# Attention in a hybrid block: one kind of score area for large query tiles, one for small ones, and the two kinds in turn

## What is computed

```python
def block(args):                      # one block of queries
    q_blk, c_blk = args
    s = jnp.einsum('bqhcd,bkhcd->bchqk', q_blk, k) * scale
    mask = cid[None, :] <= c_blk[:, None]
    p = jax.nn.softmax(jnp.where(mask, s, NEG_INF), axis=-1)
    w = p[:, 0] - lam * p[:, 1]
    return jnp.einsum('bhqk,bkhe->bqhe', w, v)
```

## Time and profile before

| | us |
|---|---|
| median of 3 timed runs | 2460.54 |
| lowest, highest of them | 2460.26, 2462.5 |
| profiled execution, span | 2463.3 |
| attention in it | 351.0 to 567.0 |
| TensorE busy, whole span | 2234.1 (91%) |
| VectorE, ScalarE, GpSimd busy | 776.3, 475.8, 308.1 |

### The profile page before, as it was taken

How to read it: one execution, slowest core, us unless ns; L and a number is a source line. 1 busy time by engine, 2 the same in 40 slices (tenths; PEclk the granted TensorE clock), 3 DMA queues, 4 the chain that set the end, 5 groups by cost and what they waited for, 6 DMA issues and landing times. The chain is left out here.

```text
span 2463.3 us, 33586 instructions
## 1 busy us (share of the span) xinstructions
PE 2234.1 (91%) x13475; PEld 1269.7 (52%) x13475; DVE 776.3 (32%) x1637; ACT 475.8 (19%) x884; POOL 308.1 (13%) x263
## 2 busy tenths in 40 slices
PE   5999978889968999999976999999986999999994
PEld 4687535565545455455533555555544555545541
DVE  5652026554352111111116344444233111111116
ACT  2222114341110000000003344442110000001001
POOL 5343000001101111101003000000100101111102
PEclk9999988789978999999988999999987999999997
DMA  4100010002229999989979211102118999998987
GB/s 152 36 4 32 17 71 1 1 1 57 72 104 390 419 419 420 419 335 406 412 298 310 93 39 38 38 19 54 52 51 350 413 419 420 420 389 353 417 369 293
DMA packets 148201, 529.82 MB, mean 215 GB/s; under 512 B 43875, under 2 KB 66947, under 8 KB 131665
## 3 DMA queue, kind: packets, MB, share of 16 engines
q1 hardware_dynamic: 119232, 490.78, 50.4%
q0 software_dynamic: 13312, 33.84, 3.6%
q10 hardware_dynamic: 15504, 3.08, 0.6%
HBM read 499.99 MB, written 39.98 MB: 219 GB/s over the span
## 5 line engine op out<-in xcount | busy, mean ns | idle before, releaser
L1787 PE MATMUL l_main_pgu<-l_w_ring,l_ex_xT 128*64 128x256 f32 (+1 forms) x4992 | 472.8, 384 | 12.7 <-DMA l_w_ring<-in_l_moe_w_gate 9.5
L1787 PEld LDWEIGHTS l_main_pgu<-l_w_ring,l_ex_xT 128*64 128x64 f32 (+1 forms) x4992 | 285.2, 128 | 189.6 <-issue 40.5
L1833 PE MATMUL l_main_py<-l_w_ring,l_ex_hT 128*64 128x512 f32 (+1 forms) x1248 | 231.9, 595 | 1.9 <-DVE l_ex_hT L1904 1.9
L1784 PE MATMUL l_main_pgu<-l_w_ring,l_ex_xT 128*128 128x512 f32 x384 | 170.1, 596 | 4.8 <-DMA l_w_ring<-in_l_moe_w_gate 4.8
L2245 PE MATMUL lru_pr<-h2T,lru_wz 128*128 128x352 f32 (+1 forms) x480 | 144.3, 461 | 11.6 <-ACTq L2300 11.6
L1900 DVE TENSOR_TENSOR l_ex_hid<-l_ex_sil,l_main_pgu 128x256 f32<-128x256 f32 (+1 forms) x76 | 35.2, 463 | 376.9 <-PE l_main_pgu L1787 279.7
L1904 DVE COPY l_ex_hT<-l_main_ph 128x256 f32<-128x256 f32 (+1 forms) x76 | 35.4, 466 | 366.4 <-PE l_main_ph L1808 366.4
L2263 PE MATMUL lru_pg<-h2T,lru_wz 128*128 128x512 f32 x320 | 148.7, 592 | 0.0
L1833 PEld LDWEIGHTS l_main_py<-l_w_ring,l_ex_hT 128*64 128x64 f32 (+1 forms) x1248 | 69.1, 127 | 132.1 <-issue 124.8
L2245 PEld LDWEIGHTS lru_pr<-h2T,lru_wz 128*128 128x128 f32 x480 | 92.6, 193 | 64.4 <-ACTq L2300 12.0
L1876 ACT ACTIVATE l_ex_sil<-l_main_pgu 128x256 f32<-128x256 f32 (+1 forms) x76 | 31.7, 417 | 468.9 <-PE l_main_pgu L1787 373.2
(11 more groups left out here) (450 smaller groups left out, 2785.2 us busy)
## 6 DMA issues: line engine op xcount, KB each, us to landing
l_w_ring<-in_l_moe_w_gate SPq DMA_DIRECT2D x64, 2048.0 KB, 24.4
l_w_ring<-in_l_moe_w_up SPq DMA_DIRECT2D x64, 2048.0 KB, 30.5
l_w_ring<-in_l_moe_w_down SPq DMA_DIRECT2D x64, 2048.0 KB, 32.5
l_y<-expert_rows SPq DMA_DIRECT2D x32, 512.0 KB, 8.3
h_rows<-H SPq DMA_DIRECT2D x24, 512.0 KB, 5.2
lru_wz<-in_l_w_in SPq DMA_DIRECT2D x20, 512.0 KB, 5.0
H<-h_rows SPq DMA_DIRECT2D x16, 512.0 KB, 10.1
w_in<-in_l_w_in SPq DMA_DIRECT2D x3, 2048.0 KB, 8.1
```

What stands on the lines that cost most here:

```text
L1784: last = pe.matmul(out[:], x[:, k, :], w[0][:, k, :], start=k == 0, stop=k == KD - 1)
L1787: last = pe.matmul(out[HALF * h + o:HALF * h + o + m, 0:256], x[:, k, it.at + o:it.at + o + m], w[n][:, k, 256 * h:256 * h + 256], start=k ...
L1833: last = pe.matmul(py[b][HALF * h + o:HALF * h + o + m, :], hT[:, c % 2, HALF * (c // 2) + o:HALF * (c // 2) + o + m], ws[n][:, c, 512 * h ...
```

## The change

- The units are put in a new order: a list of wide units (tiles 4 to 8 in heads 0 and 2, 8 to 5 in heads 1 and 3) and a list of narrow ones (3 to 0, and 0 to 4) are dealt in turn, 18 of each.
- PSUM is divided anew: one area of two maps by 1024 columns for the units of even number, one of two maps by 512 columns for those of odd number. Scores of u now wait for both exponentials of u-2.
- Keys over an area's end (tile 8 in a wide area, tile 4 in a narrow one) go to the last 16 columns of the other area, beside the scores of the unit before, whose keys don't reach so far. TensorE does this ahead of that unit's scores; VectorE copies them out ahead of that unit's minima. Six units have such a tail, where four had one before.
- The waits around the tail in the bank `weighed` go.
- Of a tailed unit ScalarE takes the tail's exponential first.
- Lambda is made behind the first unit's minima and exponentials.

The orders of turn, weigh, copies, output and square against each other are as before.

```diff
-    WIDE, PER = 1024, 4
-    units = [(hd, qi) for hd in range(HEADS - 1) for qi in range(NT)] + [(HEADS - 1, qi) for qi in reversed(range(NT))]
+    WIDE, NARROW, PER = 1024, 512, 4
+    wide = [(hd, qi) for hd in range(HEADS) for qi in ((4, 5, 6, 7, 8) if hd % 2 == 0 else (8, 7, 6, 5))]
+    narrow = [(hd, qi) for hd in range(HEADS) for qi in ((3, 2, 1, 0) if hd % 2 == 0 else (0, 1, 2, 3, 4))]
+    units = [unit for two in zip(wide, narrow) for unit in two]
     U = len(units)
+    room = [(WIDE, NARROW)[u % 2] for u in range(U)]
+    keys = [sum(TILES[qi]) for _, qi in units]
+    held = [min(n, r) for n, r in zip(keys, room)]
+    tailed = [n > r for n, r in zip(keys, room)]
...
-        S = [ctx.enter_context(nc.psum_tensor(f"scores{i}", [P, WIDE], F32)) for i in range(3)]
+        S = [ctx.enter_context(nc.psum_tensor(f"scores{i}", [P, 2, n], F32)) for i, n in enumerate((WIDE, NARROW))]
...
+        tail_place = lambda u, m: S[(u - 1) % 2][0:m, :, room[u - 1] - N_META:room[u - 1]]
...
             def scores(u):
-                if u:
-                    pe.wait_ge(exp_done, 2 * u - 1)
-                if n > WIDE and u > LAG + 1:
-                    pe.wait_ge(o_copied, u - LAG - 1)
...
+                if u >= 2:
+                    pe.wait_ge(exp_done, 2 * u - 2)
+                if u >= 2 and tailed[u - 1]:
+                    pe.wait_ge(tail_done, tails[u])
+                if u + 1 < U and tailed[u + 1]:
+                    tail_scores(u + 1)
...
+            def tail_scores(u):
...
+                for c in range(2):
+                    pe.matmul(place[:, c, :], K.qT[rows[c], hd, q0:q0 + m], K.kT[rows[c], hd, h:n], start=True, stop=False)
+                for c in range(2):
+                    pe.matmul(place[:, c, :], hide[rows[c], 0:m], ones[rows[c], 0:n - h], start=False, stop=True).then_inc(tail_made, 1)
...
-                if j == 0 and tails[min(u + LAG + 2, U)]:
-                    pe.wait_ge(tail_done, tails[min(u + LAG + 2, U)])
...
         @block.scalar
-            act.wait_ge(lam_ready, 2)
-            act.activation(lexp[:], ldot[:], ACT.Exp).then_inc(lexp_done, 1)
...
+                if u == -1:
+                    act.wait_ge(lam_ready, 2)
+                    act.activation(lexp[:], ldot[:], ACT.Exp).then_inc(lexp_done, 1)
...
         @block.vector
+            def copy_tail(u):
+                m = TILES[units[u][1]][1]
+                dve.wait_ge(tail_made, 2 * tails[u + 1])
+                dve.wait_ge(s_ready, 2 * u)
+                if tails[u]:
+                    dve.wait_ge(exp_done, 2 * last_tail(u) + 2)
+                dve.tensor_copy(tail_sb[0:m, :, :], tail_place(u, m)).then_inc(tail_done, 1)
+                dve.wait_ge(tail_done, tails[u + 1])
...
             for u in range(-1, U + LAG + 1):
+                if u + 2 < U and tailed[u + 2]:
+                    copy_tail(u + 2)
                 if u + 1 < U:
                     minimum(u + 1, 0)
                     minimum(u + 1, 1)
+                if u == -1:
+                    difference()
                 if 0 <= u < U:
                     combine(u)
```

More of the change, by code:

```diff
@@ L657, in attention @@
     ms_ready, sd_ready, on_ready, oT_ready, oT_copied, g_ready = map(sem, ("ms_ready", "sd_ready", "on_ready", "oT_ready", "oT_copied", "g_ready"))
-    WIDE, PER = 1024, 4
-    units = [(hd, qi) for hd in range(HEADS - 1) for qi in range(NT)] + [(HEADS - 1, qi) for qi in reversed(range(NT))]
+    WIDE, NARROW, PER = 1024, 512, 4
+    wide = [(hd, qi) for hd in range(HEADS) for qi in ((4, 5, 6, 7, 8) if hd % 2 == 0 else (8, 7, 6, 5))]
+    narrow = [(hd, qi) for hd in range(HEADS) for qi in ((3, 2, 1, 0) if hd % 2 == 0 else (0, 1, 2, 3, 4))]
+    units = [unit for two in zip(wide, narrow) for unit in two]
     U = len(units)
+    room = [(WIDE, NARROW)[u % 2] for u in range(U)]
+    keys = [sum(TILES[qi]) for _, qi in units]
+    held = [min(n, r) for n, r in zip(keys, room)]
+    tailed = [n > r for n, r in zip(keys, room)]
+    assert U == HEADS * NT and not tailed[0]
+    assert all(keys[u] <= room[u] + N_META and keys[u - 1] <= room[u - 1] - N_META for u in range(U) if tailed[u])
     groups = [-(-(qi + 1) // PER) for _, qi in units]
     first_group = [sum(groups[:u]) for u in range(U + 1)]
-    tails = [sum(qi == NT - 1 for _, qi in units[:u]) for u in range(U + 1)]
+    tails = [sum(tailed[:u]) for u in range(U + 1)]
+    last_tail = lambda u: max(v for v in range(u) if tailed[v])
     with ExitStack() as ctx:
-        S = [ctx.enter_context(nc.psum_tensor(f"scores{i}", [P, WIDE], F32)) for i in range(3)]
+        S = [ctx.enter_context(nc.psum_tensor(f"scores{i}", [P, 2, n], F32)) for i, n in enumerate((WIDE, NARROW))]
         tp = ctx.enter_context(nc.psum_tensor("turned_w", [P, PER, P], F32))
         out_bank = ctx.enter_context(nc.psum_tensor("weighed", [P, 512], F32))
-        po, tail = out_bank[:, 0:P], out_bank[:, P:P + 2 * N_META].rearrange("p (c n) -> p c n", c=2)
+        po = out_bank[:, 0:P]
+        tail_place = lambda u, m: S[(u - 1) % 2][0:m, :, room[u - 1] - N_META:room[u - 1]]
         block = ctx.enter_context(nc.Block())
@@ L691, in cuts @@
             q0, m = TILES[units[u][1]]
-            n = q0 + m
-            ends = list(range(0, n, 512)) + [n]
-            return q0, m, n, list(zip(ends, ends[1:]))
+            return q0, m, keys[u], held[u]
         @block.tensor
@@ L698, in _ @@
             pe.wait_ge(hide_made, 4)
+            rows = [slice(64 * c, 64 * c + 64) for c in range(2)]
             def scores(u):
                 hd, qi = units[u]
-                q0, m, n, parts = cuts(u)
-                if u:
-                    pe.wait_ge(exp_done, 2 * u - 1)
-                if n > WIDE and u > LAG + 1:
-                    pe.wait_ge(o_copied, u - LAG - 1)
-                rows = [slice(64 * c, 64 * c + 64) for c in range(2)]
-                if n > WIDE:
-                    for c in range(2):
[L711 to L720, removed]
+                q0, m, n, h = cuts(u)
+                if u >= 2:
[4 more added lines that the diff above has]
+                    tail_scores(u + 1)
+                seen = n - 64 if qi else n
+                ends = list(range(0, h, 512)) + [h]
+                for a, b in reversed(list(zip(ends, ends[1:]))):
+                    lo = max(a, seen)
+                    for c in range(2):
+                        last = pe.matmul(S[u % 2][0:m, c, a:b], K.qT[rows[c], hd, q0:q0 + m], K.kT[rows[c], hd, a:b], start=True, stop=lo >= b)
                         if lo >= b and a == 0:
@@ L724, in scores @@
                         for c in range(2):
-                            last = pe.matmul(place(c, lo, b), hide[rows[c], 0:m], ones[rows[c], 0:b - lo], start=False, stop=True)
+                            last = pe.matmul(S[u % 2][0:m, c, lo:b], hide[rows[c], 0:m], ones[rows[c], 0:b - lo], start=False, stop=True)
                             if a == 0:
                                 last.then_inc(s_ready, 1)
+            def tail_scores(u):
+                hd, qi = units[u]
+                q0, m, n, h = cuts(u)
+                place = tail_place(u, m)
+                for c in range(2):
+                    pe.matmul(place[:, c, :], K.qT[rows[c], hd, q0:q0 + m], K.kT[rows[c], hd, h:n], start=True, stop=False)
+                for c in range(2):
+                    pe.matmul(place[:, c, :], hide[rows[c], 0:m], ones[rows[c], 0:n - h], start=False, stop=True).then_inc(tail_made, 1)
             def turn(u, j):
@@ L771, in _ @@
                 for h in range(HEADS):
-                    last = pe.transpose(S[i % 2][:, P * h:P * h + m], o_sb[0:m, i, P * h:P * h + P], K.ident[0:m, 0:m])
+                    last = pe.transpose(S[i % 2][:, 0, P * h:P * h + m], o_sb[0:m, i, P * h:P * h + P], K.ident[0:m, 0:m])
                 last.then_inc(oT_ready, 1)
@@ L804, in exps @@
                 act.wait_ge(mn_ready, x + 1)
-                s, prob, kw = S[x % 3], probs[u % PROBS][c], dict(bias=mn[0:m, x % 4:x % 4 + 1], scale=-1.0)
-                if n <= WIDE:
-                    act.activation(prob[0:m, 0:n], s[0:m, 0:n], ACT.Exp, accum_out=l[0:m, u % PROBS, c:c + 1], **kw).then_inc(exp_done, 1)
-                else:
-                    act.activation(prob[0:m, 0:WIDE], s[0:m, :], ACT.Exp, accum_out=l2[0:m, tails[u] % 2, c, 0:1], **kw)
-                    act.activation(prob[0:m, WIDE:n], tail_sb[0:m, c, :], ACT.Exp, accum_out=l2[0:m, tails[u] % 2, c, 1:2], **kw).then_inc(exp_done, 1)
+                s, prob, kw = S[u % 2], probs[u % PROBS][c], dict(bias=mn[0:m, x % 4:x % 4 + 1], scale=-1.0)
+                if not tailed[u]:
+                    act.activation(prob[0:m, 0:n], s[0:m, c, 0:n], ACT.Exp, accum_out=l[0:m, u % PROBS, c:c + 1], **kw).then_inc(exp_done, 1)
+                else:
+                    act.activation(prob[0:m, h:n], tail_sb[0:m, c, :], ACT.Exp, accum_out=l2[0:m, u % PROBS, c, 1:2], **kw)
```

(27 more changed lines are left out.)

6 lines of the change are left out of this document (3 added, 3 removed).

## The result

The kernel after takes 2475.8 us (median of 4 runs, 2471.4 to 2477.5) against 2460.9 us; the ratio is 1.0062 [1.0048, 1.0076]. I had forecast 2452 us. The second rival had 2474 us. Executions of one and the same kernel differ too, in most by up to 14 us, and they are longer where the granted clock, as a mean over the whole span, is lower: of 60 of the kernel before the shortest span is 2451.6 us at 0.949, the longest 2465.1 us at 0.942. One of the ten executions of after_fill took 5953.7 us at a granted clock of 0.41; the ratio leaves it out.

What follows compares the result with a forecast made beforehand. TensorE was taken to bound the attention loop, waiting mostly for turned-weight copies. Walk to 532.0 us plus 15 for the clock gave loop end 547.0 against 555.6, -8.6 us, so 2452 us; range 2440 to 2472.

Steps and rivals of the forecast that it cites:

- The second rival: Heavy pairs: output copy behind ScalarE's second exponential idles TensorE, clock stays 1.2 GHz, costing 37 us: 2474 us; chance 0.28.
- What bounds the loop: Attention loop: 19.6 us of TensorE waits for turned-weight copies outweigh the 5.8 us, outside the start, that a second area removes.
- Start: Loop start: lambda later puts scores of units 0 to 2 before 360.5 us; unit 4's scores end at 373.5.
- The walk of the pairs at full clock: Steady loop at 2.4 GHz: nine pair periods sum to 83.6 us, 41.8 per head against 40.6 before; no gain.
- The pair walked as 8.3 us: Lighter loop pair, wide units of 784 then 912 keys, ScalarE owning the first copy: 8.3 us per period.
- the one walked as 7.0: First of the nine walked loop periods, c = 4 in tile numbers: 7.0 us.
- The new wait of the weighing: Loop: weighing waits for the narrow unit's output copy behind ScalarE's second exponential, 1 us and over, about ten times.
- Drain: Loop end: the last units have 656 and 528 keys, taking 15 us against about 8 before.
- Clock: Loop: TensorE's clock drops behind idle stretches, six falls of 2.5 us, 15 us in all; bounds 8 and 37.
- The grant below 0.75 over the loop: Sign that the forecast is wrong: TensorE's granted clock below 0.75 over the whole attention loop.
- The first, no change: Loop: clock's share is 18 to 28 us as lighter pairs fall too; 2455.5 to 2465 us, middle 2460; chance 0.30.
- The third: Much faster: all waits hung on the areas, TensorE runs dense, 18 pairs of 6.9 us: 2406 us; chance 0.04.

Runs made afterwards that it cites:

- after_fill: Kernel after plus 26 unread float32 matmuls on TensorE ahead of the second turns of wide units, in their waits: 2454.0 us, ratio 0.9971.
- order_only: Kernel before with only the new order of units; its three areas, tails and start stay: 2495.7 us, ratio 1.0123.
- after_out_early: Kernel after with ScalarE's output copy ahead of the second exponential instead of behind it: 2462.0 us, ratio 1.0015.
- after_lambda_first: Kernel after with lambda made ahead of the first minima, as in the kernel before: 2480.8 us, ratio 1.0082.

## Why the prediction was wrong

- *What bounds the loop, and that its order is the matter*: right. Waits for the turned copy, not for areas; order_only shows it by itself (35.1 us of waits for the copy, 19.6 before).
- *Start*: right. Unit 4's scores end at 373.8 us (373.5); taking the edit out raises the median by 5 us, a size that the intervals leave uncertain.
- *The walk of the pairs at full clock*: nearly right. The pair walked as 8.3 us takes 8.9 (from 436.7 to 445.6), the one walked as 7.0 takes 7.6 (from 470.0 to 477.6); the turn and the weighing of the heavy pair are within 0.4 us. The new wait of the weighing was named, as 1 us and over some ten times; it came six times, 0.55 to 1.24 us, 5.4 us in all.
- *Drain*: walked as 15 us, measured 23.8, at a grant of 0.57. At 1.00, in after_fill, it takes 17.6 us, so the walk was 2.6 us short and the clock cost 6:
```profile
529.20:546.80 17.60, 13.68 (x86) 9.68 (x84) 10.52 (x37) 7.37 (x23) 0.00 (x0) 1.00 0.00 0
```
- *Clock*: **this is the step that failed**, "I take six falls of 2.5 us", 15 us. There are twelve falls, and most last 7 us, two of them 17 and over 20. Fifteen periods took 177.7 us where the walk has 143.5, and the drain adds 8.8: together 43 us over the walk in place of 15, and 547.0 + 28 is the measured 575.2. In these stretches 102 us ran at half. At the 0.33 us for each that after_fill gives, the clock's share is about 34 us; the other 9 are the walk, too short at full clock as the pairs and the drain above show. The 0.35 us for each that I took for the old loop was about right: what was wrong is how often and how long the grant falls. I had counted the idle stretches nearly right (ten of 1.6 us or more) and then let four of them pass without a fall; the control in my own sum, that the old loop had lost 21 us behind shorter waits, should have weighed more. I had let the 5 us of unbroken work behind a fall end it at once, when the row for 499 to 503 us showed half clock in a stretch of unbroken work. The grant below 0.75 over the loop, which I had named as a sign of being wrong, came (0.73).
- *Rivals*: the second gave the time (2474) and nearly the clock's share (37 us for some 34), and in after_out_early its mechanism is shown for 12 to 14 us. But it put the whole on the output copy. The runs put more on the waits for the turned copy: filling these is worth 22 us with the output copy left where it is. The first, no change, put the clock at 18 to 28 us and ended at 2465, too low. The third had no part in it; its sum names 18 pairs of 6.9 us but adds 117, which is 17 of them.

## What to carry to other kernels

An order that moves short work away from a wait has two prices: the wait, and the clock of what comes behind it; here the second was the larger, and a walk of the waits alone gave no sign of it. Where the walk can't remove a wait of TensorE, try matmuls sized to the wait in it: here they cost nothing inside it, and one place later they cost their length. And look at the order of an in-order queue (an output copy ahead of a long exponential) where the waits name it: it gave 12 to 17 us in the new order, where the weighing waited for the copy, and nothing in the old one.

## What the runs showed of the hardware that I had not expected

- A microsecond at half clock cost about 0.3 us: 28.4 us of the loop for 86 between the kernel after and after_fill, and 0.30 by the 60 executions of the kernel before.
- In the kernel after, behind the loop's fill, the grant fell behind every wait of TensorE of 1.64 us and over, and behind two of 1.32 us.
- Work behind a wait raised the grant two thirds as much as work in it (0.85 against 0.92, from 0.73).
- The grant stayed at half for 17 us of nearly unbroken matmuls in the kernel after (449 to 466 us), and came back in some 4 us at the same place of after_out_early. It is no chance of one execution: after_lambda_first, with the same order, has 0.50 from 451 to 467 us with TensorE busy for all of it. What makes the difference was not tried further.
